# Eight experts written out one after another, and their router weights spread over the partitions before the first of them

## The reference

```
logits = einsum('bld,de->ble', h, w_router)
top_val, top_idx = top_k(logits, 2);  gate = softmax(top_val)
combine = gate scattered to the 8 experts, 0 elsewhere
for e in range(8):
    act = silu(h @ w_gate[e]) * (h @ w_up[e])
    out = out + combine[..., e:e + 1] * (act @ w_down[e])
```

## Time and profile before

| what | value |
|---|---|
| median of three runs (lowest to highest) | 2083.34 us (2074.75 to 2088.03) |
| the profiled execution: its own time / its span | 2086.81 us / 2085.0 us |
| mean granted TensorE clock, share of full speed | 0.962 |
| PE busy, share of the span | 1972.3 us, 95% |
| DVE / ACT / POOL busy | 1233.6 / 983.7 / 300.4 us |
| layer 1's experts, first matmul to last sum added to x | 1260.27 to 2071.7 us |

### The profile page before, as it was taken

One profiled execution on the slowest core, in us unless ns is written; L12 is line 12 of the kernel. 1 busy time (PEld: TensorE's weight loads), 2 busy tenths in 40 slices (PEclk: granted clock), 3 DMA queues, 4 the chain that ended last, 5 costly groups with the idle time before them and its releaser, 6 DMA issues.

```text
span 2085.0 us, 38416 instructions
## 1 busy us (share of the span) xinstructions
PE 1972.3 (95%) x15601; PEld 1898.1 (91%) x15601; DVE 1233.6 (59%) x1862; ACT 983.7 (47%) x1613; POOL 300.4 (14%) x294
## 2 busy tenths in 40 slices
PE   6999999998999989999999979999999899989997
PEld 5999989987899979998999868999999899989997
DVE  5665755533565676658654245666566656656665
ACT  4445445533554544544544344545454445444544
POOL 4952231000000059323300000000000000000000
PEclk9999969998999999999899988999999999999999
DMA  6543435477345445434443863554454535453543
GB/s 260 194 167 140 146 119 182 162 267 287 143 162 196 146 174 185 182 119 163 155 172 142 311 234 122 173 183 167 161 180 169 193 140 186 162 191 131 203 157 118
DMA packets 64472, 367.12 MB, mean 176 GB/s; under 512 B 7348, under 2 KB 12020, under 8 KB 32180
## 3 DMA queue, kind: packets, MB, share of 16 engines
q1 hardware_dynamic: 62260, 358.07, 48.1%
q0 software_dynamic: 2048, 6.62, 0.9%
HBM read 340.19 MB, written 24.48 MB: 175 GB/s over the span
## 4 chain that ended last, share of the span: by engine, by line
PE 84%; DVE 7%; DMA 4%; ACT 3%; issue 2%; SPq 0%; DVEq 0%; ACTq 0%
PE ps L543 24%; PE ps L544 24%; PE ps L545 24%; PE ps L529 2%; PE ps L782 2%; DMA ring<-w_v_dram 1%; PE ps L763 1%; DVE wL L322 1%; DVE stream L1634 1%; DMA ring<-w_o_dram 1%; PE ps L799 1%; ACT wH L316 1%; DVE proj L1691 1%; DVE tmp L1409 1%; DMA ring<-w_gu_dram 1%
## 5 line engine op out<-in xcount | busy, mean ns | idle before, releaser
L322 DVE TENSOR_TENSOR wL<-ring,wH 128x1024 fp32r<-128x1024 f32 x591 | 733.4, 1243 | 492.1 <-ACT wH L316 489.4
L543 PE MATMUL ps<-hH,wH 128*128 128x264 f32 x2784 | 804.6, 289 | 25.4 <-DVE wL L322 15.7
L544 PE MATMUL ps<-hL,wH 128*128 128x264 f32 x2784 | 795.8, 286 | 8.1 <-issue 8.1
L545 PE MATMUL ps<-hH,wL 128*128 128x264 f32 x2784 | 794.7, 285 | 0.0
L316 ACT ACTIVATE wH<-ring 128x1024 fp32r<-128x1024 f32 x591 | 621.8, 1055 | 309.8 <-PE ps L545 263.3
L543 PEld LDWEIGHTS ps<-hH,wH 128*128 128x128 f32 x2784 | 531.3, 191 | 37.1 <-issue 22.0
L544 PEld LDWEIGHTS ps<-hL,wH 128*128 128x128 f32 x2784 | 531.4, 191 | 9.5 <-issue 9.0
L545 PEld LDWEIGHTS ps<-hH,wL 128*128 128x128 f32 x2784 | 528.8, 190 | 0.0
L543 PE MATMUL ps<-projR,wH 128*128 128x264 f32 (+1 forms) x1520 | 435.2, 286 | 10.9 <-DVE projR L1752 5.9
L544 PE MATMUL ps<-projR,wH 128*128 128x264 f32 (+1 forms) x1520 | 432.4, 284 | 0.0
L545 PE MATMUL ps<-projR,wL 128*128 128x264 f32 (+1 forms) x1520 | 432.3, 284 | 0.0
(11 more groups left out here) (291 smaller groups left out, 1705.8 us busy)
## 6 DMA issues: line engine op xcount, KB each, us to landing
ring<-w_gu_dram SPq DMA_DIRECT2D x110, 1024.0 KB, 4.8
ring<-w_in_dram SPq DMA_DIRECT2D x58, 1024.0 KB, 4.8
ring<-w_down_dram SPq DMA_DIRECT2D x80, 704.0 KB, 4.1
stream<-states_dram SPq DMA_DIRECT2D x32, 512.0 KB, 4.3
ring<-w_out_dram SPq DMA_DIRECT2D x16, 1024.0 KB, 4.9
o_states_dram<-stream SPq DMA_DIRECT2D x32, 512.0 KB, 4.3
ring<-kc_dram SPq DMA_DIRECT2D x16, 1024.0 KB, 6.4
ring<-vc_dram SPq DMA_DIRECT2D x16, 1024.0 KB, 7.7
```

Of the source, the lines that this page charges most:

```text
L322: dve.tensor_tensor(wL[:, buf * PIECE:(buf + 1) * PIECE], slot(s, half * PIECE, PIECE), f32(wH[:, buf * PIECE:(buf + 1) * PIECE]), ALU.sub ...
L543: pe.matmul(dst, wh, high(k0 + k), start=k0 + k == 0, stop=False)
L544: pe.matmul(dst, wh, low(k0 + k), start=False, stop=False)
L545: ins = pe.matmul(dst, wl, high(k0 + k), start=False, stop=k0 + k == k_all - 1)
```

## The change

The loop is gone: each engine's stream holds all eight experts of layer 1 one behind another, with constants in the waits, and SP loads plain addresses. The two empty places behind each pair are gone too, so blocks go round the four slots without a break; layer 1's `w_in` starts in slot 2 instead of slot 0.

The router's rows are spread in front of the first expert: eight fp32 matmuls on PE, each with a column of the identity repeated 128 times as weights (so that row e of `combT` reaches every partition), into PSUM banks 6 and 7 in turn, and eight copies on ACT into eight tiles `combB[e]` in a free part of `proj`. From the third on, a matmul waits until ACT has copied the one two before it. DVE's mask (line 1836), PE's matmul inside each expert (line 1022) and DVE's copy (line 1842) are gone. On ACT the eight copies stand behind the wait for the layer's output transfers and ahead of the first piece that ACT splits within the first expert.

```diff
-PAIR_BLOCKS, PAIR_EMPTY = 2 * (GU_BLOCKS + DOWN_BLOCKS), 2
-PAIR_PIECES = 2 * PAIR_BLOCKS
+EXPERT_BLOCKS = GU_BLOCKS + DOWN_BLOCKS
+EXPERT_PIECES = 2 * EXPERT_BLOCKS
...
     def block(self):
-        if self.at in EMPTY_PLACES:
-            self.at += PAIR_EMPTY
         s = self.at % SLOTS
...
-ROUNDS = [1, NE // 2]
+EXPERTS = (2, NE)
...
-        combT, combM, combB = conv[0:8, 1024:1024 + NT], conv[0:8, 1300:1300 + NT], conv[:, 1600:1600 + NT]
+        combT, combB = conv[0:8, 1024:1024 + NT], [tile(proj, 2 * F_TILES + e) for e in range(NE)]
...
# SyncE
-                        sp.wait_ge(lo_ready, r.i * r.pieces + max(free[s][1], wrap))
+                if free[s]:
+                    sp.wait_ge(*free[s])
...
-                    with sp.Fori(0, ROUNDS[l]) as i:
-                        r.i = i
-                        for e in range(2):
-                            expert(i * 2 + (2 + e), e == 0)
+                for e in range(EXPERTS[l]):
+                    expert(sum(EXPERTS[0:l]) + e)
...
# TensorE
-                        if moe and f == 0:
-                            pe.wait_ge(ex_mask, at(1, ee + 1))
-                            pe.matmul(bank(6, 0, NT), ones[0:NE, :], combM, start=True, stop=True).then_inc(ex_bc, 1)
...
-                rounds(pe, r, l, expert)
+                if moe:
+                    for e in range(NE):
+                        if e >= 2:
+                            pe.wait_ge(ex_bc_in, e - 1)
+                        pe.matmul(bank(6 + e % 2, 0, NT), ident[0:NE, e:e + 1].to_broadcast([NE, P]), combT, start=True, stop=True).then_inc(ex_bc, 1)
+                for ee in range(EXPERTS[l]):
+                    expert(ee)
...
# ScalarE
                 act.wait_ge(dma_out, 16 * OUTS * (l + 1))
+                if l % 2 == 1:
+                    for e in range(NE):
+                        act.wait_ge(ex_bc, e + 1)
+                        act.activation(combB[e], bank(6 + e % 2, 0, NT), ACT.Copy).then_inc(ex_bc_in, 1)
...
# VectorE
-                    if moe:
-                        dve.tensor_scalar(combM, combT, const[0:NE, bass.ds(i * 2 + (C_ID + ee), 1)], None, ALU.mult).then_inc(ex_mask, 1)
...
                         if moe and f == 0:
-                            dve.wait_ge(ex_bc, at(1, ee + 1))
-                            st(dve.tensor_copy(combB, bank(6, 0, NT)))
+                            dve.wait_ge(ex_bc_in, ee + 1)
...
-                            st(dve.tensor_tensor(sg, sg, combB, ALU.mult))
+                            st(dve.tensor_tensor(sg, sg, combB[ee], ALU.mult))
```

More of the change, by code:

```diff
@@ L82, in __call__ @@
         ins.then_inc(self.sem, 1)
[L83 to L90, removed]
+        self.eng.wait_ge(self.sem, self.n)
 class Ring:
     def __init__(self):
-        self.used, self.at, self.piece, self.i, self.half = [0] * SLOTS, 0, 0, None, 0
+        self.used, self.at, self.piece, self.half = [0] * SLOTS, 0, 0, 0
     def block(self):
-        if self.at in EMPTY_PLACES:
-            self.at += PAIR_EMPTY
         s = self.at % SLOTS
         self.at, self.used[s] = self.at + 1, self.used[s] + 1
-        return s, self.before(s)
-    def before(self, s):
-        return self.used[s] - 1 if self.i is None else self.i * self.per[s] + (self.used[s] - 1)
+        return s, self.used[s] - 1
     def next_piece(self):
@@ L116, in next_piece @@
                 self.block()
-            self.s, _ = self.block()
-        q = self.piece if self.i is None else self.i * self.pieces + self.piece
-        out = self.s, self.before(self.s), self.half, q, self.piece % BUFS
+            self.s, self.before = self.block()
+        out = self.s, self.before, self.half, self.piece, self.piece % BUFS
         self.half, self.piece = 1 - self.half, self.piece + 1
         return out
[L123 to L136, removed]
 ATTEND = "kkwk" + "kkwk" + "kkwv" + "vvwv" + "vvvv"
-LAYER_PLACES = [IN_BLOCKS + KT + 2 * 4 + len(ATTEND) + 4 + PAIR_BLOCKS + PAIR_EMPTY for l in range(DEPTH)]
+EXPERTS = (2, NE)
+LAYER_PLACES = [IN_BLOCKS + KT + 2 * 4 + len(ATTEND) + 4 + EXPERTS[l] * EXPERT_BLOCKS for l in range(DEPTH)]
 ATTEND_AT = [sum(LAYER_PLACES[0:l]) + IN_BLOCKS + KT + 2 * 4 for l in range(DEPTH)]
 CACHE_PLACES = [at + n for at in ATTEND_AT for n, kind in enumerate(ATTEND) if kind != "w"]
-EMPTY_PLACES = [sum(LAYER_PLACES[0:l + 1]) - PAIR_EMPTY for l in range(DEPTH)]
-ROUNDS = [1, NE // 2]
[L148 to L155, removed]
-            r.i = i
[L157 to L163, removed]
 def program(nc, t):
@@ L424, in load_state, with expert @@
                 sp.dma_start(state(u), t["states"][l, u]).then_inc(state_in[u % STATE_SLOTS], 16)
-            def expert(e, first):
-                gu, down = (t[k].rearrange("e b p n -> p (e b) n") for k in ("w_gu", "w_down"))
+            def expert(e):
                 for j in range(GU_BLOCKS):
-                    load(gu[:, bass.ds(e * GU_BLOCKS + j, 1), :], wrap=wraps[j] if first and j < SLOTS else 0)
+                    load(t["w_gu"][e, j])
                 for j in range(DOWN_BLOCKS):
-                    load(down[:, bass.ds(e * DOWN_BLOCKS + j, 1), :], F_TILES * P)
+                    load(t["w_down"][e, j], F_TILES * P)
             for l in range(DEPTH):
@@ L1007, in _, with expert @@
                     pe.wait_ge(lin_free[n % 2], n // 2 + 1)
[L1009 to L1012 removed]
+                def expert(ee):
                     gu0, dn0 = l * 2 * F_TILES + ee * F_TILES, l * 2 * KT + ee * KT
@@ L1388, in expert @@
                             split_high(act, r)
-                rounds(act, r, l, expert)
+                for ee in range(EXPERTS[l]):
+                    expert(ee)
                 act.preload_act_table_set("natural_log_exp_and_others")
@@ L1852, in expert @@
                             split_low(dve, r)
-                        dve.wait_ge(piece_done, at(PAIR_PIECES // 2, q0 + 2 * F_TILES + 2 * j + 2))
+                        dve.wait_ge(piece_done, q0 + 2 * F_TILES + 2 * j + 2)
                         dve.tensor_tensor(tile(xT, j), tile(xT, j), bank(4 + j % 2, 0, NT), ALU.add).then_inc(down_free, 1)
-                rounds(dve, r, l, expert, st, 2 * (F_TILES + 1))
+                for ee in range(EXPERTS[l]):
+                    expert(ee)
                 dve.wait_ge(down_free, (2 * KT, 2 * KT + NE * KT)[l])
```

67 lines of the change are left out of this document (20 added, 47 removed).

## The result

The changed kernel takes 2049.69 us (median of four runs, 2047.44 to 2052.02) against 2083.76 of the kernel before in the same comparison: a ratio of 0.9842, 95% interval 0.9807 to 0.9878, 34.1 us less. The prediction said 2047, range 2037 to 2062.

The account below looks back on a forecast made before the run. The prediction took PE's unbroken run of matmuls, with some holes, as the bound. Its terms, 32.6 + 6.6 - 5 + 2 = 36.2 us, off a median of 2083.3 gave 2047 us, range 2037 to 2062.

Parts of the forecast that it names:

- Part 1: At the loop's three returns in layer 1: late weight loads leave PE idle or slow; removal saves 32.6 us.
- the return's pause stays in part: Rival at the old returns: code fetch still pauses PE 2.5 us each, perhaps lowering the clock; 2055 to 2069 us, chance 0.08.
- the loop was free: Rival at the returns: the hole comes from changing down to gate blocks, the jump adds little; some 2079 us, chance 0.03.
- Part 2: Inside each layer 1 expert: removing the mask and its matmul saves 0.83 us, eight times, 6.6 us.
- Part 3: In front of the first expert: the eight spread matmuls stand on PE's path and lose 5 us, bounds 3.8 to 9.
- the rival without overlap: In the spread: PE and ACT take turns at low clock, costing 10 to 12 us; 2052 to 2054 us, chance 0.08.
- Part 4: At both layers' ends: earlier `w_in` loads end ACT's wait before the last split, saving 1.0 us each, 2 us.
- Slower by a falling clock: Rival in the written-out experts: TensorE loses clock without pauses; 2114 us at mean clock 0.92, chance 0.03.

Follow-up runs that it names:

- both cures: The kernel before, loop and empty places kept, with ten tiny matmuls ahead of the loop and each round's third and later loads held: 2060.89 us.

## Why the prediction was right, and where it was not

**Part 1, 32.6 us: the size held, the reason did not.** The seven intervals fell by 38.4 us, as the two terms say for seven (32.6 + 7 x 0.83). The size was a difference of measured intervals, and the change took away loop and empty places together, so it came out whichever of them was to blame; in that the prediction was lucky. The step that failed is "The cause stands in SP's queue ... the first two blocks of a round come too late". The loads were late, but PE had its pieces: with the empty places kept and the loop gone no interval grew. What PE waited for was its own code, which the prediction had as an addition only. The misreading began at a row: the profile put PE's 4.5 us down to DVE's split, because the wait's semaphore counts pieces and a later split fell into the idle time. The piece that PE needed had been split well before PE ran dry at 1455.9; it is this one in the trace before, on DVE's timeline:

```profile
1453.15 1.23 DVE L322 TENSOR_TENSOR wL<-ring,wH 128x1024 fp32r<-128x1024 f32 x1 [2.25 <-ACT wH L316]
```

DVE is three pieces ahead: counted back from the pair's last sum, this is the first piece of the next round. The kernel before shows it by itself: at its third return PE starts while the split that was named at the first is still under way (it starts at 1867.73 and takes 1.22 us), and there the same pause is put down to issue:

```profile
1868.89 0.39 PE L543 MATMUL ps<-hH,wH 128*128 128x264 f32 x1 [4.37 <-issue]
```

The empty places did matter in the loop, by another way: they made four loads start at the time of the jump (DMA share 1.03 in the earlier trace rows), and the code, which the page counts on the same 16 DMA engines, came late.

**The rival "the return's pause stays in part" fell**, and by its own argument against: in the written-out experts PE's code came in without a pause in 764.30 us, 50 packets on q8. The Trainium skill, Runtime: NRT & Kernel Launch, Instruction fetch mechanics, says that code is fetched in blocks of 16 KiB, in sequence, and that a taken branch to a block not held stalls. The trace agrees: three packets of 0.05 MB together at a return, pauses of 2.0 us at best. The rival "the loop was free" fell: a return cost 10.5 to 11.2 us before and 2.0 at the least with both cures.

**Part 2, 6.6 us: right.** 96.73 to 95.91, eight times.

**Part 3, 5 us: too small.** The first product came 7.2 us later than before, and so did the first sum (6.4 + the first mask's 0.83). The term was taken near its low end because "the sums over partitions, which are such matmuls, reach full pace within 3.3 us". The reading of the sums holds (the row is cut off by its window; all 16 took 5.33 us), but they are not such matmuls: they have 128 rows, the spreads eight. With 128 rows the clock rose under the spreads and 3.1 us came back. It was inside the bounds (7.2 was named for the case that the spreads do not warm the clock). The lower bound was summed wrongly: 5.0 + 1.6 us of spreads save the 5.0 - 2.8 = 2.2 us that the products lost at half clock, so it is 4.4, not 3.8; with 128 rows the loss was 75.78 - (72.50 - 0.83) = 4.1. The overlap with ACT was as expected: at half clock PE sets the pace, some 0.9 us a spread, so the rival without overlap fell.

**Part 4, 2 us: 1.6 measured**, 0.7 behind layer 0 and 0.9 behind layer 1, by the reason given; the late loads cost something only there.

**Slower by a falling clock:** fell; 764 us at 1.00.

Together 36.2 were predicted and 34.1 came; 2.2 less by the spread and 0.4 less by the ends would account for that within half a microsecond. So close a fit is chance: the interval of the ratio leaves 25 to 40 us open, and four runs of the kernel before lie up to 13 us apart. The intervals, which repeat to a hundredth, carry the argument.

## What to carry to other kernels

A term that is a difference of two measured stretches stands even if its story is wrong, but the story decides what to do next: with the loop kept, holding back loads took 14.2 us off the three returns, moving the loop's code by 40 instructions 12.4, and both 24.7 of the 32.6, in one run each. Before a wait is put down to its named releaser, count which item the waiting engine needs and look when that one was ready. Where a hardware loop surrounds a busy matmul stream, price its return by the idle time at the boundary, and look at what the DMA engines carry at that moment.

## What the runs showed of the hardware that was not expected

- At a return of PE's loop 2.0 to 2.3 us passed between two starts of matmuls where the loads were held, and 4.1 to 5.1 where the DMA engines were at full share (1.01 to 1.03). A second pause, seven matmuls later, took 1.9 to 3.6 us; 40 instructions ahead of the loop removed it.
- Matmuls of eight rows did not raise the clock in 7.4 us; the same matmuls with 128 rows, 120 of them against zeros, had it at full after 5.1 us. In one run, with short waits for ACT between them, the clock fell from full under those of eight rows.
- The same first 600 us of code took 6.4 us more in one profiled execution than in the other, at a mean clock of 0.95 and 0.96.
